# A two-block fp32 kernel on one core: HGRN exponentials in PSUM, modulation products in four column groups, head norm by Ln and Exp

## What is computed

```python
mod_l = (jax.nn.silu(c) @ w_mod[l] + b_mod[l])[:, None, :]          # 1024 -> 6144, for c and for c_ctx
pl = _modulate(_rmsnorm(xl, norm1_w[l]), sh1, sc1) @ w_in[l]
...
def step(S, inp):                                                   # _hgrn_scan, chunks, 4 heads, two directions
    b = jnp.cumsum(fc, axis=2)
    rel = jnp.where(causal, b[:, :, :, None, :] - b[:, :, None, :, :], -jnp.inf)
    a = jnp.einsum('bhtk,bhtsk,bhsk->bhts', qc, jnp.exp(rel), kc)
    o = jnp.einsum('bhts,bhsv->bhtv', a, vc) + jnp.einsum('bhtk,bhkv->bhtv', qc * jnp.exp(b), S)
    S_new = jnp.exp(bL)[..., None] * S + jnp.einsum('bhsk,bhsv->bhkv', kc * jnp.exp(bL[:, :, None] - b), vc)
...
out = lambda h, g: (_head_rmsnorm(h, norm_w) * jax.nn.silu(g))      # after both directions are added
```

## Time and profile before

| | us |
|---|---|
| median of 3 runs (3337.09 to 3339.12) | 3337.84 |
| the profiled execution, its own time | 3338.61 |
| its span, first to last instruction | 3336.5 |
| PE busy in the span | 3232.4 |
| DVE, ACT, POOL busy | 1428.7, 585.1, 2076.2 |
| first modulation on PE | 24.95 to 54.5 |
| HGRN stage, from PE's first level product to the last output product | 452.5 to 630.3 |

### The profile page before, as it was taken

How to read it: one execution, slowest core, us unless ns; L and a number is a source line. 1 busy time by engine, 2 the same in 40 slices (tenths; PEclk the granted TensorE clock), 3 DMA queues, 4 the chain that set the end, 5 groups by cost and what they waited for, 6 DMA issues and landing times.

```text
span 3336.5 us, 39832 instructions
## 1 busy us (share of the span) xinstructions
PE 3232.4 (97%) x15087; PEld 2597.2 (78%) x15087; DVE 1428.7 (43%) x1672; ACT 585.1 (18%) x925; POOL 2076.2 (62%) x1483
## 2 busy tenths in 40 slices
PE   4999989899999999999999999999999999999998
PEld 2867965678888888887788888888888767888887
DVE  4844257669843432234434333233312434343321
ACT  3144234222211110011201110011001221021100
POOL 2442445568887776754467777777767435677764
PEclk8989988899999999999999999999999999999999
DMA  6120222322223322331132332332334212233232
GB/s 195 45 64 26 64 69 89 101 88 89 96 87 107 99 90 86 103 124 64 51 99 90 101 101 81 95 107 94 93 92 128 76 51 83 93 101 100 89 87 78
DMA packets 350003, 298.24 MB, mean 89 GB/s; under 512 B 6596, under 2 KB 347588, under 8 KB 349640
## 3 DMA queue, kind: packets, MB, share of 16 engines
q1 hardware_dynamic: 346616, 290.49, 27.8%
q10 hardware_dynamic: 3280, 6.26, 0.6%
HBM read 292.53 MB, written 2.10 MB: 88 GB/s over the span
## 4 chain that ended last, share of the span: by engine, by line
PE 91%; DVE 5%; POOL 2%; issue 1%; ACT 1%; DMA 0%; DVEq 0%; SPq 0%; POOLq 0%; ACTq 0%
PE pm L1960 24%; PE pm L1962 23%; PE pm L1961 23%; PE pm L2131 3%; DVE cacc L1313 2%; PE pa L1960 2%; PE pa L1962 2%; PE pa L1961 2%; PE pa L2278 1%; PE pa L2435 1%; PE pa L2448 1%; POOL wlo L584 1%; PE pm L2224 1%; PE pm L2006 1%; PE pm L2007 1%
## 5 line engine op out<-in xcount | busy, mean ns | idle before, releaser
L584 POOL TENSOR_TENSOR wlo<-raw,whi 128x512 fp32r<-128x512 f32 (+1 forms) x1096 | 1440.3, 1344 | 22.9
L580 POOL TENSOR_SCALAR whi<-raw 128x2048 fp32r<-128x2048 f32 (+1 forms) x274 | 483.8, 1766 | 1117.1 <-PE pm L1962 642.7
L1960 PE MATMUL pm<-hh,whi 128*128 128x512 f32 x2408 | 946.8, 393 | 24.3 <-DVE hl L1269 21.0
L1962 PE MATMUL pm<-hh,wlo 128*128 128x512 f32 x2408 | 939.1, 390 | 0.0
L1961 PE MATMUL pm<-hl,whi 128*128 128x512 f32 x2408 | 939.1, 390 | 0.0
L1960 PEld LDWEIGHTS pm<-hh,whi 128*128 128x128 f32 x2408 | 453.4, 188 | 128.2 <-issue 24.3
L1961 PEld LDWEIGHTS pm<-hl,whi 128*128 128x128 f32 x2408 | 453.5, 188 | 96.0 <-issue 2.4
L1962 PEld LDWEIGHTS pm<-hh,wlo 128*128 128x128 f32 x2408 | 453.2, 188 | 95.0
L1960 PE MATMUL pm<-uh,whi 128*128 128x512 f32 x880 | 342.9, 390 | 0.7 <-POOL wlo L584 0.7
L1961 PE MATMUL pm<-ul,whi 128*128 128x512 f32 x880 | 342.4, 389 | 0.0
L1962 PE MATMUL pm<-uh,wlo 128*128 128x512 f32 x880 | 342.4, 389 | 0.0
(11 more groups left out here) (415 smaller groups left out, 4121.3 us busy)
## 6 DMA issues: line engine op xcount, KB each, us to landing
raw<-in_w_ffn SPq DMA_DIRECT2D x88, 1024.0 KB, 5.3
raw<-in_w_in SPq DMA_DIRECT2D x62, 1024.0 KB, 5.2
raw<-in_w_ffn SPq DMA_DIRECT2D x64, 704.0 KB, 4.4
raw<-in_w_up SPq DMA_DIRECT2D x22, 1024.0 KB, 5.1
raw<-in_w_mod SPq DMA_DIRECT2D x20, 1024.0 KB, 5.3
raw<-in_w_out SPq DMA_DIRECT2D x12, 1024.0 KB, 5.0
raw<-in_w_down SPq DMA_DIRECT2D x16, 704.0 KB, 4.4
modraw<-in_w_mod SPq DMA_DIRECT2D x4, 1024.0 KB, 11.8
```

Source lines behind the costliest of these rows:

```text
L580: nc.gpsimd.tensor_scalar(h, r, 1.0, 1.0, ALU.mult, ALU.mult).then_inc(hi_done, 1)
L584: last = nc.gpsimd.tensor_tensor(o[:, c], r[:, c], h[:, c].bitcast(F32), ALU.subtract)
L1960: nc.tensor.matmul(out, wh, ah, start=start, stop=False)
L1962: return nc.tensor.matmul(out, wl, ah, start=False, stop=stop)
```

## The change

What it does:
- **Level exponentials.** ACT reads `yl` and writes the exponential to PSUM, `pm[1]`'s two banks in turn, and DVE's x products read it from there. POOL may overwrite `yl` when the exponentials of three levels before are done, where it waited for the x products; ACT waits for the x products of two levels before. To free the banks, the diagonal and the second modulation move to `pm[0]`, and the chunk states to `pa[2]`.
- **Modulation products.** The weights are padded to 32 columns (`silc` 128x32, zeros beside the two). Product k goes to PSUM partitions 32 (k mod 4) onward, so that each group of 32 partitions holds a sum of two products. ACT copies all 128 partitions. The turn is now a product with `modsel`, a 128x2 selection matrix that adds the four groups: 128x128 weights against two columns. DVE builds `modsel` at the start in three operations.
- **Filler order.** `MOD_REST` goes from (0, 0, 4, 3, 3, 3, 3) to (0, 0, 4, 4, 4, 4, 0).
- **Head norm.** Root and reciprocal become `Ln` and `Exp` with scale -0.5 on ACT, in the table that also serves the level exponentials and is preloaded at the stage's start. The high part is copied by ACT (`head_high`), three levels before DVE makes the low part (`hgrn_low`).
- Small things: `nought` and four small tiles move in memory, with a memset of `nought` on DVE.

```diff
@@ -66,7 +66,7 @@
-MOD_REST = (0, 0, 4, 3, 3, 3, 3)
+MOD_REST = (0, 0, 4, 4, 4, 4, 0)
...
@@ -154,7 +154,8 @@
                  [place("gated2", [P, 2, T], F32, scratch + 4 * TILE), place("gated3", [P, 2, T], F32, pad_at)]]
-        silc = place("silc", [P, KD, 2], F32)
+        silc = place("silc", [P, KD, 32], F32)
+        modsel = place("modsel", [P, 2], F32)
...
@@ -642,8 +643,7 @@
                 if lev >= 3:
-                    pool.wait_ge(hx_up, lev - 2)
-                    pool.wait_ge(hx_lo, lev - 2)
+                    pool.wait_ge(hx_exp, 2 * (lev - 2))
...
@@ -765,7 +765,13 @@
                 act.wait_ge(t_ss, h + 1)
-                nc.scalar.activation(head_sq(h), bank, ACT.Sqrt, bias=eps[:], scale=1.0 / HEAD_DIM).then_inc(t_std, 1)
+                nc.scalar.activation(head_sq(h), bank, ACT.Ln, bias=eps[:], scale=1.0 / HEAD_DIM).then_inc(t_std, 1)
+                act.wait_ge(t_std, 2 * h + 1)
+                nc.scalar.activation(head_sq(h), head_sq(h), ACT.Exp, scale=-0.5).then_inc(t_std, 1)
+
+            def head_high(h):
+                act.wait_ge(t_step, 2 * h + 2)
+                nc.scalar.activation(yh_h[:, h, 0:T], hq[:, h, :], ACT.Copy).then_inc(t_hi, 1)
...
@@ -776,7 +782,7 @@
                     act.wait_ge(mod_used, MOD_FIRST // 2 * (g + 1))
-                    nc.scalar.activation(modrow[0][:, D * g:D * g + D].rearrange("p (b n) -> p b n", b=2), pm[g][0:2, :, :], ACT.Copy).then_inc(mod_row, 1)
+                    nc.scalar.activation(modrow[0][:, D * g:D * g + D].rearrange("p (b n) -> p b n", b=2), pm[g][:], ACT.Copy).then_inc(mod_row, 1)
...
@@ -962,6 +968,7 @@
                     act.wait_ge(ctx_free[p], ctx_uses_[p])
+                nc.scalar.preload_act_table_set("natural_log_exp_and_others")
...
@@ -973,16 +980,19 @@
                     act.wait_ge(mod_used, MOD_FIRST + 2 * n + 2)
-                    nc.scalar.activation(modrow[1][:, 2 * SLAB * n:2 * SLAB * n + 2 * SLAB], pm[1][0:2, 0, :], ACT.Copy).then_inc(mod_row, 1)
+                    nc.scalar.activation(modrow[1][:, 2 * SLAB * n:2 * SLAB * n + 2 * SLAB], pm[0][:, 1, :], ACT.Copy).then_inc(mod_row, 1)
                     act.wait_ge(hy_done, lev + 1)
-                    y = halves(yl[lev % 3][:], 2 * half)
+                    if lev >= 2:
+                        act.wait_ge(hx_up, lev - 1)
+                        act.wait_ge(hx_lo, lev - 1)
+                    y, e = halves(yl[lev % 3][:], 2 * half), halves(pm[1][:, lev % 2, :], 2 * half)
                     for part, sign in ((slice(half, 2 * half), 1.0), (slice(0, half), -1.0)):
-                        nc.scalar.activation(y[:, :, part], y[:, :, part], ACT.Exp, scale=sign).then_inc(hx_exp, 1)
+                        nc.scalar.activation(e[:, :, part], y[:, :, part], ACT.Exp, scale=sign).then_inc(hx_exp, 1)
...
@@ -1001,10 +1011,13 @@
                         head_root(h - 1, pm[0][:, 0, :])
+                    if h and n % 2 == 1 and m == 4:
+                        head_high(h - 1)
                 head_root(HG_HEADS - 1, pm[0][:, 0, :])
+                head_high(HG_HEADS - 1)
...
@@ -1317,13 +1330,10 @@
-                v.wait_ge(t_std, h + 1)
-                nc.vector.reciprocal(head_sq(h), head_sq(h)).then_inc(t_step, 1)
-                v.wait_ge(t_step, 3 * h + 1)
+                v.wait_ge(t_std, 2 * h + 2)
                 nc.vector.scalar_tensor_tensor(y4[:, h, :], y4[:, h, :], cols(norm, h), head_sq(h), ALU.mult, ALU.mult).then_inc(t_step, 1)
-                v.wait_ge(t_step, 3 * h + 2)
+                v.wait_ge(t_step, 2 * h + 1)
                 nc.vector.tensor_tensor(y4[:, h, :], y4[:, h, :], gate[:, h, :], ALU.mult).then_inc(t_step, 1)
-                v.wait_ge(t_step, 3 * h + 3)
...
@@ -1491,7 +1502,8 @@
                     head_norm(h, hq, hg, "hg_norm")
-                    nc.vector.tensor_copy(yh_h[:, h, 0:T], hq[:, h, :]).then_inc(t_hi, 1)
+
+                def hgrn_low(h):
...
@@ -1517,7 +1529,7 @@
                         nc.vector.tensor_tensor(halves(xl[lev % 2][:], 2 * half)[:, :, part], halves(src, 2 * half)[:, :, part],
-                                                halves(yl[lev % 3][:], 2 * half)[:, :, part], ALU.mult).then_inc(done, 1)
+                                                halves(pm[1][:, lev % 2, :], 2 * half)[:, :, part], ALU.mult).then_inc(done, 1)
...
@@ -1526,7 +1538,7 @@
                     for u in range(5):
-                        kv = pm[0][:, 1, P * u:P * u + P] if u < 4 else pa[3][:, P:2 * P]
+                        kv = pa[2][:, P * u:P * u + P] if u < 4 else pa[3][:, P:2 * P]
...
@@ -1541,7 +1553,7 @@
                             v.wait_ge(ho_ready, h - 1)
-                        nc.vector.tensor_tensor(halves(ah[h % 2][:], P), halves(pm[1][:, 1, :], P),
+                        nc.vector.tensor_tensor(halves(ah[h % 2][:], P), halves(pm[0][:, 0, :], P),
...
@@ -1554,10 +1566,13 @@
                         hgrn_norm(h - 1)
+                    if h and m == 12:
+                        hgrn_low(h - 1)
                 hgrn_norm(HG_HEADS - 1)
+                hgrn_low(HG_HEADS - 1)
...
@@ -1569,6 +1584,10 @@
             def first():
+                nc.vector.tensor_tensor(modsel[:], ident[:, 0:2], ident[:, 32:34], ALU.add).then_inc(modsel_made, 1)
+                for g in (2, 3):
+                    v.wait_ge(modsel_made, g - 1)
+                    nc.vector.tensor_tensor(modsel[:], modsel[:], ident[:, 32 * g:32 * g + 2], ALU.add).then_inc(modsel_made, 1)
...
@@ -2120,23 +2141,25 @@
                     if i < MOD_FIRST:
-                        b, loads, out = i % len(modraw), i // len(modraw) + 1, pm[i // 4][0:2, i % 4 // 2, :]
+                        b, loads, out = i % len(modraw), i // len(modraw) + 1, pm[i // 4][:, i % 4 // 2, :]
                     else:
-                        b, loads, out = i % 2, MOD_FIRST // len(modraw) + 1 + (i - MOD_FIRST) // 2 + 1, pm[1][0:2, 0, :]
+                        b, loads, out = i % 2, MOD_FIRST // len(modraw) + 1 + (i - MOD_FIRST) // 2 + 1, pm[0][:, 1, :]
                     for k in range(KD):
-                        last = nc.tensor.matmul(out[:, SLAB * (i % 2):SLAB * (i % 2) + SLAB], silc[:, k, :], modraw[b][:, k, :], start=k == 0, stop=k == KD - 1)
+                        g = slice(32 * (k % 4), 32 * (k % 4) + 32)
+                        last = nc.tensor.matmul(out[g, SLAB * (i % 2):SLAB * (i % 2) + SLAB], silc[:, k, :], modraw[b][:, k, :], start=k < 4, stop=k >= 4)
+                pe.wait_ge(modsel_made, 3)
                 for t in range(n):
-                    last = nc.tensor.transpose(bank[:, 2 * t:2 * t + 2], row[:, P * t:P * t + P], ident[0:2, 0:2])
+                    last = nc.tensor.matmul(bank[:, 2 * t:2 * t + 2], row[:, P * t:P * t + P], modsel[:], start=True, stop=True)
...
@@ -2242,10 +2266,12 @@
                         pe.wait_ge(hd_copied, h)
+                    if h >= 2:
+                        pe.wait_ge(t_std, 2 * (h - 1))
                         for e in range(2):
-                            last = nc.tensor.matmul(pm[1][:, 1, cs], hz[e][:, h, cs], hq[:, h, cs], start=e == 0, stop=e == 1)
+                            last = nc.tensor.matmul(pm[0][:, 0, cs], hz[e][:, h, cs], hq[:, h, cs], start=e == 0, stop=e == 1)
...
@@ -2253,10 +2279,11 @@
                     pe.wait_ge(hkq, 2 * n + 2)
+                    pe.wait_ge(hd_copied, min(h + 2, HG_HEADS))
                         pe.wait_ge(pm_free[0], HG_USE + h)
-                        pe.wait_ge(t_std, h)
+                        pe.wait_ge(t_std, 2 * h)
...
@@ -2296,7 +2323,7 @@
                         for u, c in enumerate(HG_ORDER[d]):
-                            o = pm[0][:, 1, P * u:P * u + P] if u < 4 else pa[3][:, P:2 * P]
+                            o = pa[2][:, P * u:P * u + P] if u < 4 else pa[3][:, P:2 * P]
...
```

More of the change, by code:

```diff
@@ L196, in build @@
         ysq = place("ysq", [P, TT, HEAD_DIM], F32, scratch + 5 * TILE)
-        den = place("den", [P, 2, TT], F32)
-        rec = place("rec", [P, 2, TT], F32)
-        yss = place("yss", [P, TT], F32)
-        yrs = place("yrs", [P, TT], F32)
+        den = place("den", [P, 2, TT], F32, pad_at + 4160)
+        rec = place("rec", [P, 2, TT], F32, pad_at + 4224)
+        yss = place("yss", [P, TT], F32, pad_at + 4288)
+        yrs = place("yrs", [P, TT], F32, pad_at + 4352)
         cacc = [place(f"cacc{t}", [P, TA], F32, scratch + 2 * t * TILE) for t in range(2)]
@@ L744, in _ @@
             act.wait_ge(const_loaded, 16 * 4)
-            act.wait_ge(const_made, 2)
-            nc.scalar.activation(silc[:], cols("c", 0, 16).rearrange("p (k j) -> p k j", j=2), ACT.Silu).then_inc(mod_in, 1)
+            act.wait_ge(const_made, 4)
+            nc.scalar.activation(silc[:, :, 0:2], cols("c", 0, 16).rearrange("p (k j) -> p k j", j=2), ACT.Silu).then_inc(mod_in, 1)
             act.wait_ge(lb_step, 3)
@@ L1722, in ffn @@
                     return
```

(4 more changed lines are left out.)

10 lines of the change are left out of this document (6 added, 4 removed).

## The result

The changed kernel takes 3294.52 us in the median of 4 runs (3293.90 to 3295.56), the kernel before 3338.34 (4 runs) beside it: a ratio of 0.9869, 95% interval 0.9852 to 0.9886, 43.8 us less. The forecast was 3310, 28 us less; the rival of full overlap, 3286, lies nearer. In the profiled executions the span went from 3336.5 to 3292.1 us, -44.4.

| | before | after | change | forecast |
|---|---|---|---|---|
| to the end of the last slab's products, first modulation | 54.5 | 41.4 | | 41.5 |
| to the first input product | 77.7 | 66.5 | -11.2 | -10.9 |
| from there to the first level product | 374.8 | 372.0 | -2.8 | -3.5 |
| HGRN stage, first level to last output product | 177.8 | 139.5 | -38.3 | -17.6 |
| from there to the output product's first | 9.5 | 19.1 | +9.6 | +4.4 |

What follows compares the result with a forecast made beforehand. PE was taken as the bound (91% of the chain). First modulation -10.9, stage entry -3.5, stage -17.6 and second turn +4.4 gave -27.6, from 3338.6 to 3311.0, median 3310; range 3284 to 3337, the forecast's own 3292 to 3328.

Steps and rivals of the forecast that it cites:

- the rival of full overlap: Modulation products: all four column groups run side by side, a batch 0.46 us, total 3286; chance 0.20.
- the batch: Stage filler: four products take 5 record times for 8, 1.16 us each, 37.1 us in all for 59.4.
- the waits: Stage: PE waits for DVE at m=6, 0 and 1, 1.9 us per direction, 17.4 in all with the diagonal's mask.
- the clock: Stage: the same 36 us at the lower clock level as before, 14.7 us lost.
- the end of the stage: Behind the stage's last output product: the turn by selection matrix lies open, a loss of 4.4 us (2.1 to 5.5).
- the order of the records: Modulation: a group's second record runs beside the next group's first, never its own first, so 5 record times a batch.
- as a rival, 29.4: Stage: the clock stays low for twice as long, 14.7 us more, total 3325; chance 0.17.
- no better than before: Stage clock: PE busy 62% at m=6, 0 and 1, so the same 36 us at the lower level.
- Head norm and PSUM exponentials: Stage: 3.5 us gained at the entry (2.2 from x products, 1.28 from a table load), nothing more given.
- x product as 0.43 always: Stage, DVE: x products reading PSUM take 0.43 us, where from SBUF the median was 0.42 and the maximum 2.03.
- The second turn: Behind the stage: 64 records at 0.101 us, 6.5 us for 2.1; bounds 4.2 and 7.6.
- The first modulation: Start of kernel: eight slabs at 9 record times end at 41.5 for 54.5; 10.9 us gained after the turn.

Runs made afterwards that it cites:

- the spread turn: Changed kernel with the second modulation's turn spread over the HGRN stage, four blocks behind level 1 of each direction, the last four at the end: 3287.19 us.
- the last kernel: Changed kernel with the second modulation's turn spread over the stage and products that nobody reads in more of PE's idle stretches: 3275.46 us, ratio 0.9812.

## Why the prediction was right, and where it was wrong

The direction and about two thirds of the gain were right. That the time fell inside the range owes something to luck: of the sum's terms the batch (-18.9) and the waits (-11.1) came out lower than forecast, the clock (+9.3) and the end of the stage (+5.2) higher, and these errors cancel in part. With the batch alone put right, the forecast would have been 3291.

**The batch** was the largest miss: 0.57 us for 1.16, so the work at full clock fell to 109.2 us for 128.1, 18.9 more than forecast. The step that failed is the one by which a group's first record can start no earlier than the second record of the group before it. The rival with all four groups side by side was the right case (it had 0.46; the rest, 0.1 per batch, it did not have). The Trainium skill's 2.38 for three tiles (TensorE: Matmul & The Clock Gate, Part 3, Packing small matmuls) pointed the right way (by it 1.86 / 2.38 = 0.78 us a batch, which the prediction rounds to 0.75): here four tiles gave 1.86 / 0.57 = 3.3. My reason against it, the order of the records, was refuted by the pairs.

**The waits.** I expected 17.4 us; PE was idle for 6.3, an error of 11.1. The step that failed is the one that charges DVE's 5.0 us against PE's 3.1 at m=6, 0 and 1 in full. The trace has 14 waits for DVE's copies, 0.4 us in the mean, where I had 1.9 us in each of eight directions. DVE works two levels ahead of its copies, and comes out of the levels 2 to 5, each 1.6 us of PE for 1.1 of DVE, with that lead; this is read from the order of the code, and no run took the lead away.

**The clock.** I had 14.7 us of loss and, as a rival, 29.4; it was 24.0. I read the earlier trace rows rightly as a danger (the clock had fallen behind such a stretch) and then expected "no better than before". In the stretch at 486 to 490 PE was busy for 1.34 and 1.57 of 2 us, and behind it the clock was low; with unread products in these waits it did not fall there. This term eats what the filler gave: forecast's and measured stage differ by -18.9 - 11.1 + 9.3 = -20.7 us, which is 160.2 for 139.5.

**Head norm and PSUM exponentials** I gave 3.5 us at the entry (2.8 measured) and "nothing more". The runs price them at 12.8 and 6.0 alone, and at 21.6 and 37.4 as the last one in. The wrong step is that I costed them as cover over DVE in a stage bound by PE, while another paragraph of the prediction shortened PE's work: what hid DVE's 0.8 us products and 3.3 us reciprocals was the filler that the change takes away. My "x product as 0.43 always" did put this into the sum, without its price.

**The second turn** was 10.2 us for 6.5, beyond my 7.6. Its first 34 records, from 578.1 to 581.7, took 0.11 each, above the 0.101 that I took from the earlier trace rows, where I divided seven full distances and one short one by eight. The other 30 took 0.21, at the low clock:

```profile
578.00:580.00 2.00, 2.00 (x21) 2.00 (x20) 0.69 (x1) 0.63 (x1) 0.00 (x0) 1.00 0.11 37
580.00:582.00 2.00, 2.00 (x19) 2.00 (x18) 0.00 (x0) 0.00 (x0) 0.00 (x0) 0.94 0.00 0
582.00:584.00 2.00, 2.00 (x12) 2.00 (x11) 0.00 (x0) 0.00 (x0) 0.00 (x0) 0.50 0.00 0
```

That half costs 3.0 us more than at full clock, and no wait stands right ahead of it: PE's last one had ended at 575.3. In all eight kernels here that end the stage with these 64 records in one piece (the changed one and seven of the experiments), the clock fell 2 to 5 us behind their start; so the turn has a price in clock that the sum did not have. What in these products does it no run took apart. Together with a split that took 8.6 us for 7.2, the end lost 9.6 for 4.4. The split's second half took 6.3 us for 4.9; DVE's norm products of two SBUF tiles ran beside it, and before, the reciprocal did. That this is the cause was not tested.

**The first modulation** ended at 41.4, as forecast (41.5), but for another reason: not at 9 record times a slab, but at the last slab, whose load came in at 39.45 and not 38.2, and whose products ran at the low clock. The turn was 7.0 us for 3.2. That 3.8 came back behind it: from the bias to the first input product 16.9 us for 20.9, since POOL's first two splits began 12.3 us earlier (44.3 for 56.6) and DVE's norms only 7.2 earlier, so that the norms ran beside them for less time. The forecast of 10.9 for 11.2 is two errors that cancel.

Not settled: the 1.7 us behind the first output product, which no run looked at; and why a batch costs 0.1 us more than two record times. In the trace the records of a batch start together, four at 573.08 to 573.10 and four at 573.32 to 573.34, and the 0.1 lies between the latter and the level product at 573.65. That four groups and not the wider weights give the gain was not tried apart.

## What to carry to other kernels

Filler that hides another engine's waits is not free to remove: shorten it and those waits open, and the clock falls behind them, so 41 us less work on PE made the stage 1.5 us shorter alone and 19.1 with the waits gone (5.7 and 23.1 over the whole kernel). Price the parts of such a change together, in the state that they leave, and where TensorE is the bounding engine count its idle time twice, once as itself and once for the clock.

Where PE waits in short pieces and is nearly full else, look for useful work to put there first (the spread turn: 5.4 us), and then for useless work (8.9 us here).

## What the runs showed of the hardware

- Four fp32 products of 32 columns in four column groups take 0.57 us together at full clock, one group 1.86. In the order 0 0 1 1 they take 0.99: a group's records follow each other, but do not hold up another group's that stand behind them. A batch of three takes 0.56, as long as one of four.
- In the changed kernel TensorE's clock went from 2.4 to 1.2 GHz at 489.6, behind two stretches of 2 us in which PE was busy for 1.34 and 1.57, with no single wait over 0.8 us. At the stage's start it was low for 17 us (438.4 to 455.5; 14 with unread products ahead of the stage), although PE was busy nearly all the time. Products that nobody reads, put into the waits, keep it up: mean 0.93 for 0.80.
- The clock also falls while PE has no gap: inside the turns by 128x128 products against two columns, at 581.7 in the changed kernel, 3.7 us behind the turn's start, and at about 45.3 in the last kernel, 3.2 us behind it.
- A 128x128 fp32 product against two columns costs 0.11 us a record at full clock and 0.21 at the lower, about the same ratio as the level products (1.03 and 1.94 us).
